# A one-core hybrid block: memory before x at the start, branch inputs split beside the GLU, the ninth block's halves ahead of the S5 states, output rows finished one group at a time

## What is computed

```python
u = rmsnorm(x, norm_g)                       # 512 x 2048
proj = u @ w_in                              # 2048 x 13328
qkv_a, z_a, beta_raw, a_raw, x_b, z_b, q_c, z_c, gate_raw = split_columns(proj, IN_SPLITS)
p_a = (gated_deltanet(qkv_a, beta_raw, a_raw, ...) * silu(z_a)) @ w_br_a
p_b = (s5_layer(x_b, ...) * silu(z_b)) @ w_br_b          # S5, gelu, then a GLU with w_glu
p_c = (memory_cross_attention(q_c, rmsnorm(mem, mem_norm_g), w_kv_mem) * silu(z_c)) @ w_br_c
gates = sigmoid(gate_raw)                    # three of 512 x 2048
merged = gates[0] * p_a + gates[1] * p_b + gates[2] * p_c
out = rmsnorm(x + merged @ w_out, final_g)
```

## Time and profile before

| | |
|---|---|
| median of 3 runs | 2332.22 us (2330.67 to 2332.46) |
| the profiled execution | 2336.82 us, of which span 2335.0 us |
| mean granted TensorE clock | 0.984 |
| PE busy | 2222.0 us, 95% of the span |
| DVE busy | 1226.9 us, 53% |
| ACT busy | 802.6 us, 34% |
| POOL busy | 729.9 us, 31% |
| chain that ended last | PE 89%, DVE 5%, DMA 2% |

### The profile page before, as it was taken

How to read it: one execution, slowest core, us unless ns; L and a number is a source line. 1 busy time by engine, 2 the same in 40 slices (tenths; PEclk the granted TensorE clock), 3 DMA queues, 4 the chain that set the end, 5 groups by cost and what they waited for, 6 DMA issues and landing times.

```text
span 2335.0 us, 29882 instructions
## 1 busy us (share of the span) xinstructions
PE 2222.0 (95%) x10632; PEld 1792.0 (77%) x10632; DVE 1226.9 (53%) x1503; ACT 802.6 (34%) x1032; POOL 729.9 (31%) x554
## 2 busy tenths in 40 slices
PE   4999998999999999999999999999999899999996
PEld 3988786888778777777777777778777687877885
DVE  5443232257676677766766667567433334455233
ACT  6433232343343433433434334343242212123221
POOL 0000000037374483663746736457300100000000
PEclk9999998999999999999999999999999999999998
DMA  4444342433233233223333223333355445544342
GB/s 153 131 118 127 100 122 66 112 98 86 79 86 84 77 81 92 81 81 83 83 85 85 81 79 85 83 86 99 87 155 156 139 135 173 178 135 143 110 135 108
DMA packets 374343, 249.74 MB, mean 107 GB/s; under 512 B 21305, under 2 KB 349186, under 8 KB 372738
## 3 DMA queue, kind: packets, MB, share of 16 engines
q1 hardware_dynamic: 355954, 193.21, 30.2%
q0 software_dynamic: 11408, 43.00, 5.4%
q10 hardware_dynamic: 6912, 12.59, 1.5%
HBM read 221.50 MB, written 27.26 MB: 107 GB/s over the span
## 4 chain that ended last, share of the span: by engine, by line
PE 89%; DVE 5%; DMA 2%; issue 1%; ACT 1%; DVEq 0%; SPq 0%; POOLq 0%; ACTq 0%; POOL 0%
PE bank L423 26%; PE bank L425 25%; PE bank L424 25%; PE bank L855 2%; PE bank L868 2%; PE bank L938 1%; PE bank L939 1%; DVE kc L1627 1%; DVE wl L417 1%; DMA raw<-in_w_in_dram 1%; PE bank L877 1%; PE bank L760 1%; DMA xs<-in_mem_dram 1%; PE bank L947 1%; PE bank L745 0%
## 5 line engine op out<-in xcount | busy, mean ns | idle before, releaser
L423 PE MATMUL bank<-uh,wh 128*128 128x512 f32 (+1 forms) x1808 | 747.3, 413 | 34.6 <-DVE wl L417 29.7
L417 DVE TENSOR_TENSOR wl<-raw,wh 128x1024 fp32r<-128x1024 f32 x352 | 469.1, 1338 | 565.9 <-ACT wh L409 565.1
L424 PE MATMUL bank<-ul,wh 128*128 128x512 f32 (+1 forms) x1808 | 710.1, 393 | 0.0
L425 PE MATMUL bank<-uh,wl 128*128 128x512 f32 x1792 | 707.2, 395 | 0.0
L409 ACT ACTIVATE wh<-raw 128x1024 fp32r<-128x1024 f32 x352 | 370.0, 1057 | 617.3 <-DMA raw<-in_w_in_dram 217.5
L423 PEld LDWEIGHTS bank<-uh,wh 128*128 128x128 f32 (+1 forms) x1808 | 341.4, 189 | 138.8 <-issue 46.3
L425 PEld LDWEIGHTS bank<-uh,wl 128*128 128x128 f32 x1792 | 339.7, 190 | 76.3
L424 PEld LDWEIGHTS bank<-ul,wh 128*128 128x128 f32 (+1 forms) x1808 | 342.5, 189 | 67.5 <-issue 4.5
L423 PE MATMUL bank<-gh,wh 128*128 128x512 f32 x512 | 204.1, 399 | 12.2 <-DVE gl L1842 12.2
L425 PE MATMUL bank<-gh,wl 128*128 128x512 f32 x512 | 203.3, 397 | 0.0
L424 PE MATMUL bank<-gl,wh 128*128 128x512 f32 x512 | 202.4, 395 | 0.0
(11 more groups left out here) (302 smaller groups left out, 3068.2 us busy)
## 6 DMA issues: line engine op xcount, KB each, us to landing
raw<-in_w_in_dram SPq DMA_DIRECT2D x224, 512.0 KB, 3.8
raw<-in_w_kv_mem_dram SPq DMA_DIRECT2D x32, 512.0 KB, 3.8
raw<-in_w_out_dram SPq DMA_DIRECT2D x32, 512.0 KB, 3.8
gates<-gk ACTq DMA_DIRECT2D x48, 256.0 KB, 4.3
gates<-gates POOLq DMA_DIRECT2D x24, 512.0 KB, 4.5
raw<-in_s_w_glu_dram SPq DMA_DIRECT2D x16, 512.0 KB, 3.8
raw<-in_w_br_c_dram SPq DMA_DIRECT2D x16, 512.0 KB, 3.8
raw<-in_w_br_a_dram SPq DMA_DIRECT2D x16, 512.0 KB, 3.8
```

Source lines behind the costliest of these rows:

```text
L417: dve.tensor_tensor(k.wl[slot][:, c], k.raw[slot][:, c], k.wh[slot][:, c].bitcast(F32), ALU.subtract).then_inc(k.w_lo, 1)
L423: pe.matmul(o, ah, bh, start=start, stop=False)
L424: pe.matmul(o, ah, bl, start=False, stop=False)
L425: return pe.matmul(o, al, bh, start=False, stop=stop)
```

## The change

**Start.** The memory's rows are loaded first, then block 0, then x, `wba` and block 1, with no wait for `ba_tr`. The memory is scaled, transposed and split first, with block 0's split between. PE then runs blocks 0 and 1 and half of block 2. The 16 tiles of x are transposed between the following 12 eighths (`X_TILES`), and `ba` is projected three tiles behind, with high and low weights side by side in one stationary tile of 32 columns: two matmuls a tile. The squares of x are split between ACT (row groups 1 and 3) and DVE (0 and 2, in quarters). The first phase end is gone.

**Mixer.** On DVE, `split(8, 0)` and `split(8, 1)` stand before and after `s5_states(j, 3, 1)`; before, they stood behind it and behind `level_p(j, 6)`.

**GLU, branches, output.** Two phase ends are gone. The input of branch 0 is split to the first halves of `uh`, `ul` during the GLU, that of branch 1 to their second halves during branch 0, that of branch 2 to `gh`, `gl` during branch 1; tiles of `merged` are split during branch 2. The rows of x and `final_g` are loaded earlier. `hrow` is multiplied by `final_g` after each of the first three column groups. In the last one PE takes blocks 2 and 3 row group by row group, and each row group gets its own root, scaling (ACT the first 1024 columns, DVE the rest) and two stores, which SP issues.

The diff, cut to its core:

```diff
 (SyncE)
+    def rows_of_x():
+        for m in range(NT):
+            sp.dma_start(k.xs[:, MT + m, :], k.x[m * P:(m + 1) * P, :]).then_inc(k.x_in[m], 16)
+        sp.dma_start(k.wba[:, :].rearrange("p (k c) -> p k c", c=16), columns(k.w_in, BA0, 16)).then_inc(k.wba_in, 16)
...
-                if isinstance(j[0], int) and b == 0 and t == 1:
-                    sp.wait_ge(k.ba_tr, 1)
                 load_fm(k, sp, B_XA + 2 * b + t, 8, j, w, count(j, c0 + t * P, 2 * P))
+                if isinstance(j[0], int) and b == 0 and t == 0:
+                    rows_of_x()
...
+    for m in range(NT):
+        sp.wait_ge(k.fin_a, m + 1)
+        sp.dma_start(k.out[m * P:(m + 1) * P, 0:W], k.hrow[:, m, 0:W]).then_inc(k.o_st, 16)
+        sp.wait_ge(k.h_fg, 3 * NT + 2 * m + 2)
+        sp.dma_start(k.out[m * P:(m + 1) * P, W:D], k.hrow[:, m, W:D]).then_inc(k.o_st, 16)
 (GpSimd)
+    branch_load(0)
+    pool.wait_ge(k.gt_st[0], 16 * 24)
+    pool.wait_ge(k.gt_st[1], 16 * 24)
+    gate_load(0)
+    gate_load(1)
+    glu((1, 0))
+    glu((2, 0))
+    glu((3, 0))
+    pool.wait_ge(k.g_lo, KW)
+    branch_load(1)
...
 (TensorE)
+    at_big((0, 0), 0)
+    at_big((0, 0), 1)
+    at_big((0, 0), 2, range(4))
+    for q in range(4, 16):
+        for t in X_TILES[q - 4]:
+            turn_x(t)
+            if t > 2:
+                project_ba(t - 3)
+        at_big((0, 0), 2 + q // 8, [q % 8])
...
+        for kb in range(4 if c < 3 else 2):
...
+    for m in range(3):
+        for half in range(2):
+            output(3, 2, half, m)
+    for m in range(3):
+        for half in range(2):
+            mm = output(3, 3, half, m)
+        mm.then_inc(k.o_ps, 1)
+    for kb in (2, 3):
+        for half in range(2):
+            output(3, kb, half, 3).then_inc(k.w_used, 1)
+def branch_halves(k, n):
+    return [(k.uh[:, 0:KW, :], k.ul[:, 0:KW, :]), (k.uh[:, KW:KD, :], k.ul[:, KW:KD, :]), (k.gh, k.gl)][n]
 (ScalarE)
+    for b in range(KW):
+        glu((b // 2, 0), b % 2)
+        if 3 <= b < 7:
+            branch_hi(0, (2 * b - 6, 2 * b - 5))
     for n in range(3):
...
+        for b in range(KW):
+            split_hi(k, act, B_BR + KW * n + b + 1)
+            if n == 0 and 2 <= b < 6:
+                branch_hi(1, (2 * b - 4, 2 * b - 3))
+            if n == 1:
+                branch_hi(2, (b,))
+            if n == 2 and b:
+                merged_hi(2 * b - 2)
+                merged_hi(2 * b - 1)
 (VectorE)
-        if j: level_p(j, 5); level_t(j, 5); level_x(j, 6); s5_states(j, 3, 1)
+        if j: level_p(j, 5); level_t(j, 5); level_x(j, 6)
         split(8, 0)
+        if j: s5_states(j, 3, 1)
+        split(8, 1)
         if heads: convolve(a, 1)
         if j: level_p(j, 6)
-        split(8, 1)
         if heads: convolve(a, 2)
```

More of the change, by code:

```diff
@@ L730, in at_big, with turn_ba @@
+    def turn_ba():
+        pe.wait_ge(k.ba_s, 1)
+        for m in range(NT):
+            mm = pe.transpose(ps[7][:, m * 32:(m + 1) * 32], k.ba_rows[0:32, m * P:(m + 1) * P], ident[0:32, 0:32])
+        mm.then_inc(k.ba_tr, 1)
+    for t in range(KD):
+        turn_mem(t)
+    def at_big(j, b, eighths=range(8)):
         hl, n = ((k.uh, k.ul), S) if b >= 4 else ((k.mh, k.ml), MEM)
-        for q in range(8):
+        for q in eighths:
+            if isinstance(j[0], int) and j[0] == 0 and b == 0:
+                pe.wait_ge(k.m0_lo, 2 * q + 2)
@@ L1376, in scalar_program, with glu @@
     gate_out(15)
-    def glu(j):
-        for t in range(2):
+    def glu(j, *ts):
+        for t in ts:
             split_hi(k, act, B_GLU + t + 1, 2, j)
@@ L1466, in vector_program, with x_squares @@
-    end_phase(k, dve, 1)
+            ts(k.xs[:, first + m, :], k.xs[:, first + m, :], stat[:, 16 + col0 + m:17 + col0 + m], None, ALU.mult).then_inc(scaled, 1)
+    scale_rows(0, MT, 4, k.mem_root, k.mem_scale)
+    split_lo(k, dve, B_XA)
+    for t, (gain, hi, lo) in enumerate(memory_tiles(k)):
+        dve.wait_ge(k.m0_hi, t + 1)
+        stt(lo, ps[2 + t % 4][:, 0:MEM], gain, hi.bitcast(F32), ALU.mult, ALU.subtract).then_inc(k.m0_lo, 1)
+    def x_squares():
+        for m in (0, 2):
+            dve.wait_ge(k.x_in[m], 16)
+            for c in range(4):
+                row = k.xs[:, MT + m, c * S:(c + 1) * S]
+                step(stt(k.gk[c % 2][:, :], row, 1.0, row, ALU.mult, ALU.mult, accum_out=k.xss[:, m // 2, c:c + 1]))
+        dve.reduce_sum(stat[:, 0:4:2], k.xss[:, :, :], AX_X).then_inc(k.x_sq, 2)
@@ new lines, in x_rows, with x_tiles @@
+    def x_rows():
+        scale_rows(MT, NT, 0, k.x_root, k.x_scale)
+        dve.wait_ge(k.wba_hi, 1)
+        tt(k.wb[:, :, 16:32], k.wba[:, :].rearrange("p (k c) -> p k c", c=16), k.wb[:, :, 0:16].bitcast(F32), ALU.subtract).then_inc(k.wba_lo, 1)
+    def x_tiles(first, last):
+        for t, (gain, hi, lo) in list(enumerate(normed_tiles(k)))[first:last]:
+            dve.wait_ge(k.u_hi, t + 1)
+            stt(lo, ps[2 + t % 4][:, :], gain, hi.bitcast(F32), ALU.mult, ALU.subtract).then_inc(k.u_lo, 1)
@@ L1822, in vector_program, with glu @@
     split_lo(k, dve, B_GLU)
-    def glu(j):
-        for t in range(2):
+    def glu(j, *blocks):
+        for t in blocks:
             gg, zv, gv = [k.gg0, k.gg1][t], [k.zv0, k.zv1][t], [k.gv0, k.gv1][t]
@@ L1871, in vector_program, with merge @@
         tt(k.ul[:, t, :], k.merged[:, t, :], k.uh[:, t, :].bitcast(F32), ALU.subtract).then_inc(k.m_lo, 1)
+    def merge(n, b):
+        dve.wait_ge(k.gt_in[b % 2], 16 * (4 * n + b // 2 + 1))
+        for half in range(2):
+            t = 2 * b + half
+            bank = ps[4 + t % 4][:, :].unsqueeze(1)
+            gate = [k.gates0, k.gates1][b % 2][:, half:half + 1, :]
+            m = k.merged[:, t:t + 1, :]
+            dve.wait_ge(k.w_used, 2 * (B_BR + KW * n + b) + half + 1)
+            if n == 0:
+                tt(m, bank, gate, ALU.mult).then_inc(k.prod, 1)
+            else:
+                tt(gate, bank, gate, ALU.mult).then_inc(k.prod, 1)
+                dve.wait_ge(k.prod, KD * n + t + 1)
+                tt(m, m, gate, ALU.add).then_inc(k.mrg, 1)
@@ new lines, in vector_program @@
+    for b in range(KW):
+        glu((b // 2, 0), b % 2)
+        if 3 <= b < 7:
+            branch_lo(0, (2 * b - 6, 2 * b - 5))
+    for n in range(3):
+        for b in range(KW):
+            split_lo(k, dve, B_BR + KW * n + b + 1)
+            if n == 0 and 2 <= b < 6:
+                branch_lo(1, (2 * b - 4, 2 * b - 3))
+            if n == 1:
+                branch_lo(2, (b,))
+            merge(n, b)
+            if n == 2 and b:
+                merged_lo(2 * b - 2)
+                merged_lo(2 * b - 1)
```

374 lines of the change are left out of this document (191 added, 183 removed).

## The result

The changed kernel takes **2281.3 us** (median of four runs, 2279.6 to 2282.8) against 2331.4 us of the kernel before (2330.3 to 2332.5, four runs beside them): a ratio of 0.978, with an interval of 0.9768 to 0.9791. 2290.3 had been forecast, with a range of 2276 to 2303. The saving is 50.2 us where 41.9 had been summed. The profiled execution's span is 2278.5 us, 56.5 less than the 2335.0 before. A few executions, of the kernel before as of changed ones, took far longer (up to 8219 us); the ratios and intervals here leave them out.

The account below looks back on a forecast made before the run. TensorE was taken as busy almost throughout, so only idle stretches, the program's two ends and low clock could yield time: 8.5 + 4.6 + 18.5 + 10.3 = 41.9 us, from 2332.2 to 2290.3 us, range 2276 to 2303.

Parts of the forecast that it names:

- The start: Program start to end of first attention group: memory loaded first, group ends at 118.6 against 127.1, 8.5 us saved, bounds 4 and 12.
- The mixer: Ninth block's two waits in seven heads become one of 3.1 us, gone in the eighth; 4.6 us saved, bounds 2.9 and 14.5.
- So the row ends 0.4 us later: VectorE's work at a mixer head's end: ends 0.4 us later, so PE starts the next head at 933.3 instead of 934.35.
- the rival that the clock holds: Mixer: single waits of 3 us leave the clock at 2.4 GHz, the mixer gains 14.5, total 2280; chance 20%.
- The rule of the Trainium skill that was weighed: Mixer: convolution step beside GpSimd could wait out one more GpSimd operation; 0.6 us a head rather than 1.05, 3 us less.
- GLU to output: GLU, branches, output: waits before branches and output and the low clock behind them go; 18.5 us saved, bounds 14 and 19.5.
- The new wait, 0.5: GLU: gate loads queued ahead of `zv` use up the following split's 3.8 us cover; bounds 0 and 3 us, 0.5 taken.
- The end: After the last matmul: row groups finish one by one, 10.2 us for 20.5; 10.3 us saved, bounds 8 and 12.
- landing in 3.8 us like its loads of that size, and the 2 us from the last landing to the end: Program's end: SyncE's 0.5 MB stores, issued at 0.43 each, land in 3.8 us, then 2 us to the end.
- The slower case: Mixer: new wait amid small matmuls keeps the clock low; 15 us more of it in each of seven heads gives 2343; 3%.

Follow-up runs that it names:

- The experiment on the loads: Changed kernel with x's four rows and the 16 columns for `ba` loaded ahead of memory's two rows and block 0's weights: 2294.1 us, ratio 0.9833.
- that one execution: Profiled execution of the kernel before, unchanged, whose first and third branch took 233.3 ns a matmul from start to start; span 2335.0 us.

## Why the prediction was right, and where it was not

**The start: right, at 8.9 us for 8.5.** Its steps came out one by one: memory at 13.66 (13.7 forecast), split 23.30 to 25.65 (25.8), block 0 at 31.31 (31.0), block 1 at 39.95 (39.9), group end 118.15 (118.6). One step failed without weight: before block 2 PE waited 0.25 us, not 2.4, because the clock fell behind the wait before block 1 (0.91 from 40 to 60 us) and the longer block 1 absorbed it. The experiment on the loads shows what carries the term.

**The mixer: the mechanism right, the size wrong, 10.3 us for 4.6.** As the prediction put it, the wait "is not removed but moved: two become one", at the place named, in seven heads, and gone in the eighth. Three amounts were off.

- *The cost of the two old waits.* The prediction added the idle times, 2.07 + 0.49 us, to 1.6 us of low clock: 4.15 a head, and two unabsorbed falls. But an idle time of 2.07 us costs more than it reads. The timeline around the wait at 919.23 of the earlier trace rows, the matmul before it and the second one behind it:

```profile
916.77 0.39 PE L425 MATMUL bank<-uh,wl 128*128 128x512 f32 x1
...
919.57 0.40 PE L424 MATMUL bank<-ul,wh 128*128 128x512 f32 x1
```

From start to start that is 2.46 + 0.34 us where two intervals of 0.23 would do: 2.3 us for the 2.07. By such distances the heads before lost 4.6 to 4.7 us (both waits, or one wait with the fall and a rest of the second), and 6.2 in the two where no second wait absorbed the fall: 35.6 us in seven heads for the 32.4 summed, and 4.1 in the eighth for 3.8.
- *The row.* "So the row ends 0.4 us later": it ends 0.1 us earlier. From `gx` to the split of the next head's first block it took 18.54 us (913.07 to 931.61) and takes 18.41 (901.07 to 919.48). The step of v that slid beside GpSimd is there (3.26 us for three, 2.33 before), and the second half's split is shorter as forecast (1.20 for 1.72), but so is v's first step (0.92 for 1.50), which the sum left out. That step and GpSimd's operation beside it, before and after:

```profile
927.82 1.50 DVE L1624 TENSOR_SCALAR vc<-vraw,cwh 128x512 f32<-128x512 f32 x1
927.00 2.05 POOL L590 TENSOR_TENSOR gr<-gr,pt 128x512 f32<-128x512 f32 x1 [0.18 <-POOL pt L588]
914.25 1.74 POOL L600 TENSOR_TENSOR pt<-tcos,gi 128x512 f32<-128x512 f32 x1
```

In both kernels it ends 0.3 us after the GpSimd operation that was running when it began (929.3 after 929.0; 916.3 after 916.0). What differs is how much of that operation was left, 1.2 us before and 0.6 now. The moved wait costs 3.1 us from start to start (3.92 from the `weights` matmuls to the block, where 0.81 passes without a wait, 933.54 to 934.35 before), and reads 2.87.
- *The clock.* It fell in five of the seven heads, not six. A fall costs some 1.7 us here: 0.91 over 20 us is 1.8, and from one head's wait to the next 149.95 us pass behind a fall and 148.4 behind none, 1.5. Why it fell behind five of these waits and not behind the other two, which are as long, stays open.

With these, 39.7 us before against 7 x 3.1 + 5 x 1.7 = 30.2 after make 9.5 of the 10.3. Head by head, counted by their waits (the one at 919.23, called the fourth head's in the earlier trace rows, is the third, the one at 1670.52 the eighth): the first gained 3.2 us, the second to fifth nothing (149.95 us from head to head before and after; 4.7 lost before, 3.1 + 1.7 now), the sixth 1.3, the seventh 1.8, the eighth 3.8. So the rival that the clock holds was a matter of degree: in the first and the sixth it held. The seventh gained although it fell, since there a fall had stood unabsorbed before, too. The rule of the Trainium skill that was weighed ("SBUF — State Buffer", two separate sides) would have made it 0.6 a head; the trace agrees for the one step that slid (3.26 less two steps of 0.78 is 1.7 us for 0.78), while v's first step, beside GpSimd's work in both kernels, met a shorter rest of it and gave the time back.

**GLU to output: right in the waits, 24.7 us for 18.5.** Behind the stage's first wait, which both kernels have, waits and low clock lost 21.5 us before by distances from start to start, and 1.7 after: 19.8 for the 19.0 summed. The new wait, 0.5, did not come. DVE waited 5.87 us for `zv`, 3.7 more than before, as forecast; the split behind it was done at 1789.97, and PE wanted it at 1790.7 (1809.8 less the 19.1 us by which this stage starts earlier). 0.7 us of its cover were left. The other 4.9 us are the step that was missing altogether: the same number of matmuls, with no wait among them, took less time. Two branches read `uh` and not `gh`, 2 x 384 x 2.2 ns = 1.7 us; 2 x 384 x 4.4 ns = 3.4 us are the 233.3 ns of that one execution. That part can't be counted as a gain of the change, and it is about half of what the spans saved (56.5) beyond the medians (50.2).

**The end: 12.7 us for 10.3.** The order of the groups came out exactly, 3.4 us from the last matmul to the end of DVE's work. The step that failed is "landing in 3.8 us like its loads of that size, and the 2 us from the last landing to the end": 6.8 us had been put between DVE's last result and the span's end, and 4.3 passed. The 2 us fit GpSimd's stores, behind which its drain of 1.76 us stood; behind SyncE's last landing only 0.4 us passed, which makes 1.6 of the 2.5. The landing took about 3.6 us instead of 3.8, and the last store was issued 0.4 us behind DVE's result, where the sum had put both issues, 0.9, ahead of the landing.

**The slower case** asked for a clock that stays down amid small matmuls. It did not come: the window behind a fall reads 0.91, as before, so a fall lasted no longer.

## What to carry to other kernels

When one engine's row of work sets a wait, look at what stands at the row's end, not only at the instruction now waited for: moving two splits forward gave 8 to 10 us, and moving the next one ahead of a convolution, which nobody wanted yet, 28 more. Cost a wait by the distance from matmul start to matmul start and by the fall of the clock behind it, and count what absorbs that fall: a later wait on the same row does, and once it is removed the fall is paid in full. Where a wait can't be removed, cheap matmuls in it kept the clock up here and were worth 9 us.
